# Other SBUF start addresses for the streamed operands of a two-layer encoder step

## The chip, the cores and the metric

One NeuronCore of one Trainium2 chip. The time is the device time of one execution in microseconds; the metric is the median over the runs.

## The reference

Two layers of a streaming encoder on 1056 tokens (1024 of a new stream, 32 of a running one) with 1024 features. Layer 0 mixes tokens by a gated short convolution, layer 1 by windowed means. Every layer then has a squared-ReLU MLP and a gated per-layer input. All of it is float32.

```python
def trunk(x, p, ...):
    for i in range(DEPTH):                       # DEPTH = 2
        y, nh = short_conv_mixer(...) if i % 2 == 0 else pool_mixer(...)
        h = layer_norm(ALPHA * x + y, ln1_g[i], ln1_b[i])
        r = jax.nn.relu(h @ mlp_w1[i])           # 1024 -> 4096
        f = (r * r) @ mlp_w2[i]                  # 4096 -> 1024
        e = (p[i] @ ple_w[i]) * jax.nn.sigmoid(h @ ple_gate_w[i])
        x = layer_norm(ALPHA * h + f + e, ln2_g[i], ln2_b[i])
    return x, ...

def short_conv_mixer(x, hist, w_in, conv_w, w_out):
    gb, gc, h = jnp.split(x @ w_in, 3, axis=-1)  # 1024 -> 3 x 1024
    ...
    y = (gb * conv) @ w_out
```

## The kernel before

**Layout.** Features lie on the 128 partitions, tokens along the row. The 1056 tokens are cut into NG = 3 groups of TG = 352, and the 1024 features into KD = 8 blocks. `blk(t, n, k)` is the block of group n and features k: 352 floats, 1408 bytes, one behind the other without a gap.

**Products in three parts.** Each operand is held as a high part (rounded to the format that TensorE takes in one pass) and a low part (the remainder): `x_hi`/`x_lo`, `h_hi`/`h_lo`, `r_hi`/`r_lo`, and `w_split[:, slot, 0 or 1, :]` for the weights. `triple` (L696 to L701) makes a product of three matmuls into one PSUM bank: high weights with the high part (L699), high weights with the low part (L700), low weights with the high part (L701). In each of them 128 columns of weights are loaded first, and then the 352 columns of the block are streamed through the array. `full_tile` (L703) runs `triple` over the eight blocks k of a group, 24 matmuls. A block's high part is thus streamed twice, with the low part between.

**Stages.**
- Input products of the convolution: `conv_in` (L708), from x, 8 feature blocks by 3 groups by 3 outputs; its first pass for group 0 is written out in pieces (L724, L728, L734) because x is still arriving.
- Then the plan, a list of steps that all engines walk in the same order: output products (`out`), gates (`gate`), MLP up (`up`) and pool products (`grp`) stream from h; MLP down (`down`, L854) and the token inputs (`ple`, L845) stream from r. An `up` step fills one block of r: ScalarE takes relu and square and rounds to `r_hi`, VectorE subtracts to `r_lo` (L1297). A `down` step makes four output blocks, each of CHUNK = 2 triples. r has three parts of two blocks, `rpart(t, n, f)` (L583), used in turn.
- Token inputs (`p`): a load of 704 floats per partition into a buffer of `w_raw`, split into the two blocks of a part of r by one copy of ScalarE (L887) and one subtraction of VectorE (`subtract_hi`, L614).
- Weights: 512 KB loads into `w_raw` by the SP queue (L635), split into one of six slots of `w_split` by ScalarE (L889) and VectorE (L616). Plan tables (`PLACES`, `REFILL_LATER`) say at which step each refill and each piece of the layer norms stands. The change touches none of them.

**Places in SBUF.** `place` (L410) hands out byte offsets in a partition's row, from a cursor that starts at 16640, or at an offset that is given. Several tensors share a place at different times: `acc` lies on `x_hi`; the windows of the pooling (`win_0` to `win_2`), r, `t` and `y_scaled_t` lie on `x_lo`; `x_raw` and `ln_squares` lie on `h_lo`; `u`, `gc` and `conv` lie in the slots 4 and 5 of `w_split` and behind. The program before places every block and every slice of 128 weights at a multiple of 128 bytes; since 1408 = 5.5 x 256, blocks with even number start at a multiple of 256 and those with odd number 128 past one.

Of the kernel before, what the change touches and what calls it, by code (L numbers as in the profile page):

```python
# [6 lines left out]
F32 = mybir.dt.float32  # L7

F32R = mybir.dt.float32r
ALU = mybir.AluOpType  # L10
ACT = mybir.ActivationFunctionType

P = 128
# [4 lines left out]
NG = 3  # L18
TG = TOKENS // NG
TAIL = PROMPT - (NG - 1) * TG  # L20
FF = 4 * D
CHUNK = 2
NCH = FF // P // CHUNK
PLE = 256
KP = PLE // P
# [5 lines left out]
EPS = 1e-5  # L31
U = 1024
GCOLS = KD * TG

# [363 lines left out]
def bass_streaming_trunk(nc, x_t, w_stream, p_t, vectors, conv_hist, pool_hist, y_t, conv_new, pool_new):  # L400
# [6 lines left out]
    with ExitStack() as ctx:  # L407
        cursor = [-(-nc.sbuf_base // 256) * 256]

        def place(name, shape, dt, at=None):  # L410
            size = 4
            for n in shape[1:]:
                size *= n
            size = -(-size // 32) * 32
            if at is None:
                at = cursor[0]
                cursor[0] += size
            return nc.alloc_sbuf_tensor_at(name, shape, dt, offset=at), at + size
# [7 lines left out]

        big = [P, NG * GCOLS]
        at1 = cursor[0]
        xh, _ = place("x_hi", big, F32R)
        acc, _ = place("acc", big, F32, at1)  # L430
        at2 = cursor[0]
        xl, end2 = place("x_lo", big, F32R)
        at3 = at2 + -(-GCOLS * 4 // 32) * 32
        WIN = HIST + TG + HIST
        w0, at = place("win_0", [P, 2, WIN], F32, at2)
        w1, at = place("win_1", [P, 2, WIN], F32, at)
        w2, at = place("win_2", [P, 2, WIN], F32, at)
        assert at <= at3
        row_hi, at = place("row_mean_hi", [P, 2 * CHUNK, P], F32R, at2)
        row_lo, at = place("row_mean_lo", [P, 2 * CHUNK, P], F32R, at)  # L440
        row_sum, at = place("row_sum", [P, 2 * CHUNK], F32, at)
        ident, at = place("identity", [P, P], F32, at)
        diag, at = place("rstd_diagonal", [P, 3, P], F32, at)
        assert at <= at3
        rh, at = place("r_hi", [P, NG * CHUNK * TG], F32R, at3)
        rl, at = place("r_lo", [P, NG * CHUNK * TG], F32R, at)
        tt, at = place("t", [P, 2, TG], F32, at)
        gs, at = place("y_scaled_t", [P, 2, TG], F32, at)
        assert at <= end2
        hh, at6 = place("h_hi", big, F32R)  # L450
        hl, at7 = place("h_lo", big, F32R)
        xraw, _ = place("x_raw", big, F32, at6)
        squares, _ = place("ln_squares", big, F32, at6)
        ws, _ = place("w_split", [P, 6, 2, U], F32R)
        UW = CH + PROMPT + CH + SAMPLE
        CW = TG + CH
        ub, at = place("u", [P, UW], F32, at7 + 4 * 2 * U * 4)
        gcs, at = place("gc", [P, NG, TG], F32, at)
        cv, at = place("conv", [P, NG, CW], F32, at)
        assert at <= at7 + 6 * 2 * U * 4  # L460
        raw, _ = place("w_raw", [P, 4, U], F32)
        w3, _ = place("win_3", [P, 2, WIN], F32)
        ones_r, _ = place("ones_r", [P, P], F32R)
        vec, _ = place("vec", [P, NV], F32)
        zeros, _ = place("zeros", [P, 2, HIST], F32)
        chist, _ = place("conv_history", [P, KD * CH], F32)
        phist, _ = place("pool_history", [P, KD, HIST], F32)
        cnew, _ = place("conv_state", [P, KD * 2 * CH], F32)
        tails, _ = place("tails", [P, 2, KD, HIST], F32)
        ones, _ = place("ones", [P, P], F32, cursor[0] - 2 * KD * HIST * 4)  # L470
        s_mean, _ = place("sum_mean", [P, TG], F32)
        s_var, at = place("sum_var", [P, TG], F32)
        std, _ = place("std", [P, TG], F32, at - -(-TG * 4 // 32) * 32)
        var, _ = place("var", [P, TG], F32)
        rstd, _ = place("rstd", [P, TG], F32)
# [16 lines left out]
        w_hi = sem("w_hi")  # L492
# [87 lines left out]
        def f32(ap):  # L580
            return ap.bitcast(F32)

        def rpart(t, n, f):  # L583
            at = (n * CHUNK + f) * TG
            return t[:, at:at + TG]

        def vcol(at):
            return vec[:, at:at + 1]
# [21 lines left out]
        def subtract_hi(eng, u, slot):  # L610

            if isinstance(slot, tuple):
                cols = slice(slot[1] * KP * TG, (slot[1] + 1) * KP * TG)
                ins = eng.tensor_tensor(rl[:, cols], raw[:, u.q, 0:KP * TG], f32(rh[:, cols]), ALU.subtract)  # L614
            else:
                ins = eng.tensor_tensor(ws[:, slot, 1, :], raw[:, u.q, :], f32(ws[:, slot, 0, :]), ALU.subtract)  # L616
            ins.then_inc(w_lo, 1)
# [262 lines left out]
        def _(act):  # L880
            def split_hi(u, slot, conds=()):
                act.wait_ge(raw_in[u.q], u.use * 16 + 16)
                for name, value in conds:
                    wait(act, sems[name], value)
                if isinstance(slot, tuple):
                    n = slot[1]
                    act.copy(rh[:, n * KP * TG:(n + 1) * KP * TG], raw[:, u.q, 0:KP * TG]).then_inc(w_hi, 1)  # L887
                else:
                    act.copy(ws[:, slot, 0, :], raw[:, u.q, :]).then_inc(w_hi, 1)  # L889

# [598 lines left out]
```

## Time and profile before

| | us |
|---|---|
| median of 2 runs | 2115.15 |
| lowest, highest | 2115.14, 2115.16 |
| span of the profiled execution, first to last instruction | 2114.6 |
| PE matmul busy | 2104.2 |
| PE weight load busy | 2101.3 |
| VectorE busy | 1266.8 |
| ScalarE busy | 821.8 |
| GpSimd busy | 74.8 |

The profiled execution has no time beside its span; the span is 0.5 us under the median of the runs, which also hold what lies around the instructions. The busy time of PE counts a matmul from its start to the modelled end of its results, so that consecutive matmuls overlap, and the mean duration of a group (some 320 ns) is not what one matmul costs. What one costs is seen from the starts in the timeline.

### The profile page before, as it was taken

The numbers are of one execution on the slowest core, as the hardware profiler recorded it, in microseconds if no ns is written. First come the engines' busy times: TensorE is split into PE (matmuls) and PEld (weight loads), VectorE is DVE, ScalarE is ACT, GpSimd is POOL, SyncE is SP. The second block draws the span as 40 slices with busy tenths as digits, with TensorE's granted clock in tenths as the row PEclk, the third lists the DMA queues.
The fourth block names the chain that finished last, engine by engine and source line by source line (L and its number), as shares of the span: only waits on it lengthen the run. The fifth ranks groups of instructions, "written<-read, shape, count | busy, mean of one in ns | idle before, by whom it ended". The sixth has DMA issues, their size and how long they took to land.

```text
span 2114.6 us, 31847 instructions
## 1 busy us (share of the span) xinstructions
PE 2104.2 (100%) x13214; PEld 2101.3 (99%) x13214; DVE 1266.8 (60%) x1892; ACT 821.8 (39%) x1287; POOL 74.8 (4%) x69
## 2 busy tenths in 40 slices
PE   9999999999999999999999999999999999999998
PEld 9999999999999999999999999999999999999998
DVE  5232357786454444444787877887875355645477
ACT  4222223663423322222544445555443324233345
POOL 0000000000000000000020002000300000000000
PEclk9999999999999999999999999999999999999999
DMA  4010241444122111111112343543222212122233
GB/s 175 30 60 30 69 129 48 130 129 142 63 85 96 51 50 41 40 60 41 60 54 87 100 147 120 168 139 121 62 77 92 69 51 70 51 80 80 64 107 133
DMA packets 54209, 179.68 MB, mean 85 GB/s; under 512 B 8128, under 2 KB 11328, under 8 KB 54080
## 3 DMA queue, kind: packets, MB, share of 16 engines
q1 hardware_dynamic: 51056, 177.15, 25.7%
q8 instruction: 95, 1.56, 0.3%
q10 hardware_dynamic: 3024, 0.70, 0.2%
q14 instruction: 34, 0.28, 0.0%
HBM read 173.36 MB, written 4.46 MB: 84 GB/s over the span
## 4 chain that ended last, share of the span: by engine, by line
PE 99%; DVE 0%; DMA 0%; SPq 0%; issue 0%; ACT 0%; DVEq 0%
PE ps L699 33%; PE ps L700 33%; PE ps L701 33%; DMA x_raw<-x_t 0%; DVE acc L1187 0%; PE ps L760 0%; PE ps L759 0%; PE ps L728 0%; PE ps L734 0%; SPq L641 0%; PE ps L797 0%; PE ps L724 0%; SPq L653 0%; DVE x_lo L1327 0%; SPq L649 0%
## 5 line engine op out<-in xcount | busy, mean ns | idle before, releaser
L699 PE MATMUL ps<-h_hi,w_split 128*128 128x352 f32 x2160 | 696.9, 323 | 0.4 <-DVE acc L1280 0.4
L700 PE MATMUL ps<-h_lo,w_split 128*128 128x352 f32 x2160 | 691.8, 320 | 0.0
L701 PE MATMUL ps<-h_hi,w_split 128*128 128x352 f32 x2160 | 691.6, 320 | 0.0
L699 PE MATMUL ps<-r_hi,w_split 128*128 128x352 f32 x1634 | 526.9, 322 | 0.0
L700 PE MATMUL ps<-r_lo,w_split 128*128 128x352 f32 x1634 | 523.1, 320 | 0.0
L701 PE MATMUL ps<-r_hi,w_split 128*128 128x352 f32 x1634 | 522.8, 320 | 0.0
L1311 DVE TENSOR_TENSOR acc<-acc,ps 128x352 f32<-128x352 f32 (+1 forms) x769 | 372.6, 516 | 125.5 <-PE ps L701 124.8
L616 DVE TENSOR_TENSOR w_split<-w_raw,w_split 128x1024 fp32r<-128x1024 f32 x291 | 356.5, 1247 | 99.2 <-ACT w_split L889 98.9
L699 PEld LDWEIGHTS ps<-h_hi,w_split 128*128 128x128 f32 x2160 | 405.0, 187 | 1.1 <-issue 1.0
L700 PEld LDWEIGHTS ps<-h_lo,w_split 128*128 128x128 f32 x2160 | 405.9, 188 | 0.0
L701 PEld LDWEIGHTS ps<-h_hi,w_split 128*128 128x128 f32 x2160 | 404.8, 187 | 0.0
L889 ACT CAST w_split<-w_raw 128x1024 fp32r<-128x1024 f32 x291 | 297.5, 1046 | 245.4 <-PE ps L701 243.8
L1297 DVE TENSOR_TENSOR r_lo<-t,r_hi 128x352 fp32r<-128x352 f32 x192 | 100.6, 524 | 380.0 <-ACT r_hi L1028 379.6
L700 PEld LDWEIGHTS ps<-r_lo,w_split 128*128 128x128 f32 x1634 | 306.9, 188 | 0.0
L699 PEld LDWEIGHTS ps<-r_hi,w_split 128*128 128x128 f32 x1634 | 306.4, 188 | 0.5 <-issue 0.3
L701 PEld LDWEIGHTS ps<-r_hi,w_split 128*128 128x128 f32 x1634 | 306.2, 187 | 0.0
L1022 ACT ACTIVATE t<-ps 128x352 f32<-128x352 f32 x192 | 89.3, 465 | 528.2 <-PE ps L701 526.6
L699 PE MATMUL ps<-x_hi,w_split 128*128 128x352 f32 x552 | 178.0, 322 | 0.0
L700 PE MATMUL ps<-x_lo,w_split 128*128 128x352 f32 x552 | 176.8, 320 | 0.0
L701 PE MATMUL ps<-x_hi,w_split 128*128 128x352 f32 x552 | 176.7, 320 | 0.0
L700 PEld LDWEIGHTS ps<-x_lo,w_split 128*128 128x128 f32 x552 | 103.7, 188 | 0.0
L699 PEld LDWEIGHTS ps<-x_hi,w_split 128*128 128x128 f32 x552 | 103.5, 188 | 0.0
(133 smaller groups left out, 1198.5 us busy)
## 6 DMA issues: line engine op xcount, KB each, us to landing
w_raw<-w_stream SPq DMA_DIRECT2D x315, 512.0 KB, 3.5
x_raw<-x_t SPq DMA_DIRECT2D x4, 704.0 KB, 8.7
y_t<-acc SPq DMA_DIRECT2D x4, 704.0 KB, 4.1
w_raw<-p_t SPq DMA_DIRECT2D x6, 352.0 KB, 2.8
y_t<-acc SPq DMA_DIRECT2D x7, 176.0 KB, 2.0
w_raw<-w_stream SPq DMA_DIRECT2D x3, 256.0 KB, 6.1
x_raw<-x_t SPq DMA_DIRECT2D x4, 176.0 KB, 4.5
x_raw<-x_t SPq DMA_DIRECT2D x2, 352.0 KB, 6.8
```

The source lines that it names most:

```text
L616: ins = eng.tensor_tensor(ws[:, slot, 1, :], raw[:, u.q, :], f32(ws[:, slot, 0, :]), ALU.subtract)
L699: pe.matmul(out, wh, mov_h, start=first, stop=False)
L700: pe.matmul(out, wh, mov_l, start=False, stop=False)
L701: return pe.matmul(out, wl, mov_h, start=False, stop=last)
L889: act.copy(ws[:, slot, 0, :], raw[:, u.q, :]).then_inc(w_hi, 1)
L1022: act.activation(t, ps[:, step.bank, 0:TG], ACT.Relu).then_inc(a_free, 1)
L1297: dve.tensor_tensor(rpart(rl, *r), tt[:, step.bank, :], f32(rpart(rh, *r)), ALU.subtract).then_inc(r_ready, 1)
L1311: dve.tensor_tensor(cols, cols, ps[:, bank, at:end], ALU.add).then_inc(b_free, 1)
```

## The change

It moves tensors in SBUF; what is computed, the order of instructions on each engine and the waits stay. Gaps of 64, 64, 128 and 128 bytes go in front of `x_lo`, `h_hi`, `h_lo` and `w_split`. A block of r takes RS = 368 floats (1472 bytes) of place, of which 352 are used, r begins 1024 bytes earlier within the place of `x_lo`, and `r_lo` begins 128 bytes behind the end of `r_hi`. The two instructions that fill both blocks of a part at once write through `rpair`, two runs of 352 instead of one of 704. `x_raw` and `ln_squares` move with `h_lo`.

Start of each streamed tensor in a partition, in bytes, and its remainder by 256 (even block, odd block):

| tensor | before | even, odd | after | even, odd |
|---|---|---|---|---|
| `x_hi` | 16640 | 0, 128 | 16640 | 0, 128 |
| `x_lo` | 50432 | 0, 128 | 50496 | 64, 192 |
| `h_hi` | 84224 | 0, 128 | 84352 | 128, 0 |
| `h_lo` | 118016 | 0, 128 | 118272 | 0, 128 |
| `r_hi` parts 0 and 2 | 61696 | 0, 128 | 60736 | 64, 0 |
| `r_hi` part 1 | 64512 | 0, 128 | 63680 | 192, 128 |
| `r_lo` parts 0 and 2 | 70144 | 0, 128 | 69696 | 64, 0 |
| `r_lo` part 1 | 72960 | 0, 128 | 72640 | 192, 128 |
| `w_split`, every slice of 128 weights | 151808 | 0 | 152192 | 128 |
| `w_raw`, every buffer | 200960 | 0 | 201344 | 128 |

```diff
--- before.py
+++ after.py
@@ -31,6 +31,7 @@
 EPS = 1e-5
 U = 1024
 GCOLS = KD * TG
+RS = TG + 16
 
 
 
@@ -428,9 +429,10 @@
         at1 = cursor[0]
         xh, _ = place("x_hi", big, F32R)
         acc, _ = place("acc", big, F32, at1)
+        cursor[0] += 64
         at2 = cursor[0]
         xl, end2 = place("x_lo", big, F32R)
-        at3 = at2 + -(-GCOLS * 4 // 32) * 32
+        at3 = at2 + -(-GCOLS * 4 // 32) * 32 - 1024
         WIN = HIST + TG + HIST
         w0, at = place("win_0", [P, 2, WIN], F32, at2)
         w1, at = place("win_1", [P, 2, WIN], F32, at)
@@ -442,16 +444,20 @@
         ident, at = place("identity", [P, P], F32, at)
         diag, at = place("rstd_diagonal", [P, 3, P], F32, at)
         assert at <= at3
-        rh, at = place("r_hi", [P, NG * CHUNK * TG], F32R, at3)
-        rl, at = place("r_lo", [P, NG * CHUNK * TG], F32R, at)
+        rh, at = place("r_hi", [P, NG * CHUNK * RS], F32R, at3)
+        rl, at = place("r_lo", [P, NG * CHUNK * RS], F32R, at + 128)
         tt, at = place("t", [P, 2, TG], F32, at)
         gs, at = place("y_scaled_t", [P, 2, TG], F32, at)
         assert at <= end2
+        cursor[0] += 64
         hh, at6 = place("h_hi", big, F32R)
-        hl, at7 = place("h_lo", big, F32R)
-        xraw, _ = place("x_raw", big, F32, at6)
-        squares, _ = place("ln_squares", big, F32, at6)
-        ws, _ = place("w_split", [P, 6, 2, U], F32R)
+        cursor[0] += 128
+        hl, _ = place("h_lo", big, F32R)
+        xraw, _ = place("x_raw", big, F32, at6 + 128)
+        squares, _ = place("ln_squares", big, F32, at6 + 128)
+        cursor[0] += 128
+        ws, at7 = place("w_split", [P, 6, 2, U], F32R)
+        at7 -= 6 * 2 * U * 4
         UW = CH + PROMPT + CH + SAMPLE
         CW = TG + CH
         ub, at = place("u", [P, UW], F32, at7 + 4 * 2 * U * 4)
@@ -581,8 +587,11 @@
             return ap.bitcast(F32)
 
         def rpart(t, n, f):
-            at = (n * CHUNK + f) * TG
+            at = (n * CHUNK + f) * RS
             return t[:, at:at + TG]
+
+        def rpair(t, n):
+            return t[:, n * KP * RS:(n + 1) * KP * RS].rearrange("p (k t) -> p k t", k=KP)[:, :, 0:TG]
 
         def vcol(at):
             return vec[:, at:at + 1]
@@ -610,8 +619,8 @@
         def subtract_hi(eng, u, slot):
 
             if isinstance(slot, tuple):
-                cols = slice(slot[1] * KP * TG, (slot[1] + 1) * KP * TG)
-                ins = eng.tensor_tensor(rl[:, cols], raw[:, u.q, 0:KP * TG], f32(rh[:, cols]), ALU.subtract)
+                tokens = raw[:, u.q, 0:KP * TG].rearrange("p (k t) -> p k t", k=KP)
+                ins = eng.tensor_tensor(rpair(rl, slot[1]), tokens, f32(rpair(rh, slot[1])), ALU.subtract)
             else:
                 ins = eng.tensor_tensor(ws[:, slot, 1, :], raw[:, u.q, :], f32(ws[:, slot, 0, :]), ALU.subtract)
             ins.then_inc(w_lo, 1)
@@ -884,7 +893,7 @@
                     wait(act, sems[name], value)
                 if isinstance(slot, tuple):
                     n = slot[1]
-                    act.copy(rh[:, n * KP * TG:(n + 1) * KP * TG], raw[:, u.q, 0:KP * TG]).then_inc(w_hi, 1)
+                    act.copy(rpair(rh, n), raw[:, u.q, 0:KP * TG].rearrange("p (k t) -> p k t", k=KP)).then_inc(w_hi, 1)
                 else:
                     act.copy(ws[:, slot, 0, :], raw[:, u.q, :]).then_inc(w_hi, 1)
```

## Rows read from the trace of the kernel before

**Rows 1.** The page, parts 1 and 2: busy time, and the granted clock in 40 slices.

```profile
PE 2104.2 (100%) x13214; PEld 2101.3 (99%) x13214; DVE 1266.8 (60%) x1892; ACT 821.8 (39%) x1287; POOL 74.8 (4%) x69
PEclk9999999999999999999999999999999999999999
```

**Rows 2.** The page, part 4: the chain that ended last, by engine.

```profile
PE 99%; DVE 0%; DMA 0%; SPq 0%; issue 0%; ACT 0%; DVEq 0%
```

**Rows 3.** Waits of PE, whole span: total us, times, longest.

```profile
PE ps L871 <- POOL zeros L1351: 1.1, 1, 1.1
PE ps L724 <- ACT x_hi L1052: 0.9, 1, 0.9
PE ps L790 <- DVE ln_squares L1173: 0.6, 1, 0.6
PE ps L699 <- DVE acc L1280: 0.4, 1, 0.4
PE ps L797 <- DVE rstd_diagonal L1184: 0.3, 1, 0.3
PE ps L728 <- DVE x_lo L1327: 0.2, 1, 0.2
```

**Rows 4.** The page, part 5: groups of L699, count | busy us, mean ns.

```profile
L699 PE MATMUL ps<-h_hi,w_split 128*128 128x352 f32 x2160 | 696.9, 323 | 0.4 <-DVE acc L1280 0.4
L699 PE MATMUL ps<-r_hi,w_split 128*128 128x352 f32 x1634 | 526.9, 322 | 0.0
L699 PE MATMUL ps<-x_hi,w_split 128*128 128x352 f32 x552 | 178.0, 322 | 0.0
```

**Rows 5.** Timeline of PE from 699.69 us: start us, duration us, line, operation.

```profile
699.69 0.32 PE L699 MATMUL ps<-h_hi,w_split 128*128 128x352 f32 x1
699.85 0.32 PE L700 MATMUL ps<-h_lo,w_split 128*128 128x352 f32 x1
700.01 0.32 PE L701 MATMUL ps<-h_hi,w_split 128*128 128x352 f32 x1
700.16 0.32 PE L699 MATMUL ps<-h_hi,w_split 128*128 128x352 f32 x1
700.33 0.32 PE L700 MATMUL ps<-h_lo,w_split 128*128 128x352 f32 x1
700.48 0.32 PE L701 MATMUL ps<-h_hi,w_split 128*128 128x352 f32 x1
700.64 0.32 PE L699 MATMUL ps<-h_hi,w_split 128*128 128x352 f32 x1
...
727.33 0.32 PE L699 MATMUL ps<-r_hi,w_split 128*128 128x352 f32 x1
```

**Rows 6.** Windows: 1000 to 1700 us, PE busy (x), PEld, DVE, ACT, POOL, clock.

```profile
1000.00:1700.00 700.00, 700.00 (x4404) 699.50 (x4404) 518.51 (x728) 332.50 (x522) 50.99 (x32) 1.00 0.31 99
```

**Rows 7.** Timeline of PE at the last tile: start us, duration us, line, operation.

```profile
2100.80 0.28 PE L699 MATMUL ps<-r_hi,w_split 128*128 128x256 f32 x1
...
2101.52 0.21 PE L699 MATMUL ps<-r_hi,w_split 128*128 128x96 f32 x1
2101.56 0.27 PE L700 MATMUL ps<-r_lo,w_split 128*128 128x96 f32 x1
...
2102.01 0.28 PE L701 MATMUL ps<-r_hi,w_split 128*128 128x96 f32 x1
```

**Rows 8.** Timeline of PE from 323.17 to 327.01 us, first and last row.

```profile
323.17 0.32 PE L699 MATMUL ps<-h_hi,w_split 128*128 128x352 f32 x1
...
327.01 0.32 PE L699 MATMUL ps<-h_hi,w_split 128*128 128x352 f32 x1
```

**Rows 9.** Split of the token inputs, and the weight loads (us to landing).

```profile
L887 ACT CAST r_hi<-w_raw x6: 780/780/784, 376.9 to 1594.6; 128x704 fp32r<-128x704 f32 x6
L614 DVE TENSOR_TENSOR r_lo<-w_raw,r_hi x6: 881/887/895, 381.0 to 1595.4; 128x704 fp32r<-128x704 f32 x6
w_raw<-w_stream SPq DMA_DIRECT2D x315, 512.0 KB, 3.5
```

## Prediction

> **What bounds the kernel now.** I read the page's first two parts, then the chain and the waits, to see whether any engine but TensorE sets the time. TensorE's matmul side is busy for 2104.2 of 2114.6 us, and its granted clock is 9 or more in every slice, so it runs at the 2.4 GHz level [rows 1]. The chain of waits puts 99% of the span on PE [rows 2]. PE's waits for other engines are six and sum to 3.5 us [rows 3]. VectorE (60%) and ScalarE (39%) have slack, and the kernel's only long resource is the row of 13,214 matmuls. Of these, 3 x (2160 + 1634 + 552) = 13,038 come from `triple` (L699, L700, L701), nearly all 352 columns wide: 6,480 stream h, 4,902 stream r, 1,656 stream x [rows 4].
>
> The next question is what one matmul costs. The 320 ns of the groups is no cost, since two matmuls overlap in the record; the cost is the distance from one start to the next, which I call the gap. In the timeline of one stretch [rows 5] the starts come in sets of six: three matmuls on one block (high, low, high), then three on the next. From 699.69 to 727.33 us there are 29 sets, 174 gaps: 27.64 us / 174 = 158.9 ns. Over 700 us with pooling work beside it 4404 records touch the window, two of them already running at its start, which gives 700 / 4402 = 159.0 ns [rows 6]. So the gap hardly depends on what the other engines do.
>
> 352 columns at 2.4 GHz stream in 146.7 ns, so 12.2 ns of each gap is not streaming. The last tile says what kind of time that is [rows 7]: six matmuls of 256 columns take 0.72 us, 120 ns each, against 106.7 ns of columns, so 13.3 ns over. 96 columns fewer save 38.9 ns, against 40 of pure streaming. The 12 ns is thus a cost per matmul, not per column. With 96 columns the gap is (2102.01 - 2101.56) / 4 = 112 ns, although the columns need only 40; there the weight loads set the pace. At 352 columns that pace has 47 ns to spare. 12.2 ns x 13,038 = 159 us is everything that this change could touch.
>
> **Does an address matter at all?** I averaged each of the six gaps over the 30 sets that begin from 699.69 to 727.33 us; rows 5 show the first set and the start of the last. In their order: 160.0, 161.3, 155.3, 161.7, 155.0, 159.8 ns. The second and the fifth are the same step: the low stream ends, the high one of the same block begins, with the weights' low half. They differ by 6.3 ns. What differs between the blocks is where they lie: 1408 bytes are 5.5 x 256, so even blocks start at 0 and odd ones at 128 past a multiple of 256. Address phases are worth some nanoseconds per matmul, in both directions. A second stretch warns that they are not all: between 323.17 and 327.01 us the same instructions on the same addresses go 24 gaps in 3.84 us, 160.0 ns each [rows 8]. So the same layout can run in more than one rhythm.
>
> The Trainium skill, "TensorE: Matmul & The Clock Gate", Back-to-back issue gap, gives an isolated gap of columns over 2.4 GHz plus about 2.5 ns; "SBUF — State Buffer", Who interferes with whom, gives TensorE two read ports, one for the moving operand and one for weights, and says that it never waits on anyone. By those two pages a place in SBUF is worth nothing and the time stays at 2115. The trace disagrees with the first figure (12.2 ns instead of 2.5), and the 6.3 ns between equal steps is not in the page's picture.
>
> **The change part by part.** The instruction order of all engines is the same, and so are all waits. Only two groups change shape: the six copies (L887) and six subtractions (L614) that split a token input now write two runs of 352 with 64 bytes between them instead of one of 704. They take 780 and 887 ns now [rows 9]; even twice that would be 10 us on engines with hundreds of microseconds to spare, and PE has no listed wait on them. I take nothing. If the cover were gone, the first of the six could hold PE for under a microsecond.
>
> DMA destinations: w_raw moves from a multiple of 256 to 128 past one. A load lands after 3.5 us at the median [rows 9] and loads are issued well ahead, since no wait of PE on a weight is listed [rows 3]. Nothing again; a load 1 us slower would not show.
>
> What is left is the gap, by stage.
>
> - h, 6,480 matmuls. All three of a block's streams used to start at one phase. Now the low part lies 128 off the high, and since a stream moves the phase by 128 from start to end, every matmul starts at the phase (mod 256) at which the one before it ended, and the weights keep their distance from the high part. In the old order two of six steps continue in this way, the third and the sixth: (155.3 + 159.8) / 2 = 157.6 ns. The other four mean 159.5. I take 157.6 for all: 1.25 ns x 6,480 = 8.1 us saved. Bounds: 155.0 gives 25 us saved, 161.7 gives 18 us lost.
> - r, 4,902 matmuls. Blocks start at 64 and 0, or 192 and 128, high and low parts alike, with weights at 128. The trace has no stream that starts 64 off, so I bound by its extremes: 155.0 saves 19 us, 161.7 costs 14 us. I take the middle between the best gap and the present mean, 157.0: 1.9 ns x 4,902 = 9.3 us saved. It is the weakest number here. The reason to lean to a gain is that four of the present six gaps are near the top of the seen range, so a mix of phases has more room below than above.
> - x, 1,656 matmuls. The low part is 64 off the high. Same treatment, 1.9 ns x 1,656 = 3.1 us saved; bounds 6.4 us saved, 4.7 us lost.
> - The first 19 us and the last 12 us have few matmuls and waits of another kind: nothing.
>
> Sum: 8.1 + 9.3 + 3.1 = 20.5 us saved. The span is 2114.6 us and the median of the runs 2115.15, 0.5 more, so the forecast is 2115.15 - 20.5 = 2094.6, said as 2095 us, 1.0% faster. All parts at their best: 25 + 19 + 6.4 = 50 us, 2065. All at their worst: 37 us, 2152.
>
> **Rivals.** A: *no change*. The per-matmul cost is a fixed handoff, and the rhythm settles to the same average on any layout. For it: the stage on x, the one on h and the one on r all have equal groups now (means of 322 or 323 ns at L699) [rows 4]. Against it: 6.3 ns between equal steps. It gives 2115.
>
> B: *the half line*. If a stream is fetched in pieces of 128 bytes, 1408 bytes from a multiple of 128 are 11 whole pieces, and from 64 past one they touch 12. Place: half of r's matmuls (2,451) and the third of x's that reads the low part (552). Price: at most one piece of 16 more columns, 6.7 ns, so 20 us. It decides once the 64-byte phases cost more than h gains; with h's 8.1 us kept it is 2127, with h at the slower rhythm of rows 8 (160.0, 7 us lost) 2142. I put it at 2127. For it: nothing in the trace starts on an odd 64, so nothing excludes it. Against it: at 256 columns the excess is the same as at 352, so there is no sign of a fetch that runs at its limit.
>
> C: *the best gap everywhere*. Each step falls on the phase that costs 155.0 or less: 50 us saved or more, 2065, perhaps 2060. For it: 155 is seen once in every three steps or so. Against it: the steps are coupled. A short gap (155) is always followed by a longer one in rows 5, as if the start had to wait for a turn that comes round; then an average near the minimum needs every step to fit.
>
> The Trainium skill, "SBUF — State Buffer", Specifications, says lines are 16 bytes and each crossing costs. All starts here, old and new, are multiples of 64 bytes and all streams contiguous, so by it B is excluded too; no row tests it.
>
> **How the numbers follow.** Forecast (a gain of 0.2 to 2%) 0.44; A 0.20; B (any loss over 0.2%) 0.20, of which 0.04 over 2%; C 0.16. About 2% is what a measurement of this kernel can tell from no change. Faster by over 2% (below 2073) is C, 0.16; slower by over 2% (above 2157) needs more than the worst gap seen, at most 0.04; within 2% is the rest, 0.80. For eight in ten I go from 2066, where C's bulk lies, to 2128, just past B.
>
> **What would show it.** Right for h: in the timeline of a stretch on h the six gaps become equal or alternate in two values, with a mean below 158.9. Right for r and x: the same sets of six below 158.9. B: gaps of L700 on x_lo, and of r's first blocks, up by some nanoseconds while their odd partners stay. A: sets of six at 953 to 960 ns in all three stages. Wrong altogether: a new wait on PE, for r_lo, x_lo or a weight, or a clock below 9 in a slice. Stages may go opposite ways; the sum of three signs is what this rests on.

## The result, and the profile after

The changed kernel takes 2140.03 us (median of 2 runs, 2139.28 to 2140.77) against 2115.15: ratio 1.0119, 95% interval 1.0094 to 1.0143. It is 1.2% slower, where 1.0% faster was forecast, and it lies above the range's end of 2128. A second series beside the kernel before gave 2141.05 against 2116.00 us, ratio 1.0118 (1.0101 to 1.0135).

The page of the changed kernel, parts 1, 2 and 4, in the order of [rows 1, 2]:

```profile
span 2139.0 us, 31847 instructions
PE 2128.6 (100%) x13214; PEld 2126.3 (99%) x13214; DVE 1269.7 (59%) x1892; ACT 822.4 (38%) x1287; POOL 74.9 (3%) x69
PEclk9999999999999999999999999999999999999999
PE 99%; DVE 0%; DMA 0%; SPq 0%; issue 0%; ACT 0%; DVEq 0%
```

Nothing else became a bound: PE holds 99% of the chain as before, the clock is the same, and the waits of PE sum to 3.4 us (3.5 before). VectorE and ScalarE are busy for 3 and 1 us more. Three of PE's waits, from the list (total us, times, longest):

```profile
PE ps L733 <- ACT x_hi L1061: 0.5, 1, 0.5
PE ps L708 <- DVE acc L1289: 0.4, 1, 0.4
PE ps L733 <- DVE w_split L1334: 0.3, 1, 0.3
```

The last of them, on the weights' first pieces, was not in the list before, and the prediction had named a new wait on a weight as a sign of being wrong. It is 0.3 us, on the line (L733, L724 before) that waited 0.9 us for x_hi before and waits 0.5 us for it now, so it adds nothing.

The copies into the two runs of r were to cost nothing, and did: L623 is L614 of before, where its mean was 888 ns.

```profile
L623 DVE TENSOR_TENSOR r_lo<-w_raw,r_hi 128x704 fp32r<-128x704 f32 x6 | 5.3, 887 | 1.0 <-ACT r_hi L896 1.0
```

The time is in the gaps. Windows of the changed kernel, PE busy (x records), then PE's weight loads and the other engines in the same form, the granted clock, the DMA share and GB/s; the three stretches are input products (x), output products (h), and a mix of h and r:

```profile
100.00:280.00 180.00, 180.00 (x1120) 180.00 (x1119) 59.42 (x102) 39.08 (x63) 11.79 (x15) 1.00 0.13 47
300.00:370.00 70.00, 70.00 (x435) 70.00 (x434) 52.13 (x66) 23.02 (x26) 0.00 (x0) 1.00 0.25 81
1000.00:1700.00 700.00, 700.00 (x4353) 699.71 (x4352) 516.83 (x723) 330.72 (x519) 51.09 (x32) 1.00 0.30 99
```

The first two windows in the kernel before:

```profile
100.00:280.00 180.00, 180.00 (x1135) 180.00 (x1134) 60.21 (x105) 39.31 (x64) 11.91 (x16) 1.00 0.14 47
300.00:370.00 70.00, 70.00 (x439) 70.00 (x439) 53.45 (x69) 22.49 (x26) 0.00 (x0) 1.00 0.23 74
```

With the two matmuls that already run at a window's start left out, the stage on x went from 180 us / 1133 = 158.9 ns per matmul to 180 / 1118 = 161.0, and the mix from 159.0 [rows 6] to 700 / 4351 = 160.9. From 300 to 370 us, h alone, it is 70 / 433 = 161.7. In the kernel before this stretch is one of the slower ones on h, 70 / 437 = 160.2, where the mean over all of h is 159.0. The starts show this without counting. In the timeline of the stage on x, 25 sets of six lie between the first row and the last, 24.16 us / 150 = 161.1 ns; a set takes 0.966 us where it took 0.953 [rows 5]:

```profile
100.18 0.33 PE L709 MATMUL ps<-x_lo,w_split 128*128 128x352 f32 x1
100.34 0.33 PE L710 MATMUL ps<-x_hi,w_split 128*128 128x352 f32 x1
100.50 0.32 PE L708 MATMUL ps<-x_hi,w_split 128*128 128x352 f32 x1
100.66 0.32 PE L709 MATMUL ps<-x_lo,w_split 128*128 128x352 f32 x1
100.82 0.32 PE L710 MATMUL ps<-x_hi,w_split 128*128 128x352 f32 x1
100.99 0.32 PE L708 MATMUL ps<-x_hi,w_split 128*128 128x352 f32 x1
101.14 0.33 PE L709 MATMUL ps<-x_lo,w_split 128*128 128x352 f32 x1
...
124.34 0.33 PE L709 MATMUL ps<-x_lo,w_split 128*128 128x352 f32 x1
```

On h, 144 gaps in 23.28 us are 161.7 ns:

```profile
318.16 0.32 PE L708 MATMUL ps<-h_hi,w_split 128*128 128x352 f32 x1
...
341.44 0.32 PE L710 MATMUL ps<-h_hi,w_split 128*128 128x352 f32 x1
```

Here is the loss by stage, each mean taken over all starts of the stage in the trace (gaps above 205 ns left out), before and after: x 158.9 and 161.1, h 159.0 and 161.6, r 158.9 and 160.0. Times 1,656, 6,480 and 4,902 matmuls this is 3.6 + 17.0 + 5.4 = 26.0 us; the long gaps (above 205 ns, at waits) sum to 1.6 us less. The spans differ by 24.4.

The groups of part 5 hide it almost wholly, since each duration covers two matmuls [rows 4]:

```profile
L708 PE MATMUL ps<-h_hi,w_split 128*128 128x352 f32 x2160 | 699.0, 324 | 0.4 <-DVE acc L1289 0.4
L708 PE MATMUL ps<-r_hi,w_split 128*128 128x352 f32 x1634 | 527.5, 323 | 0.0
L708 PE MATMUL ps<-x_hi,w_split 128*128 128x352 f32 x552 | 177.9, 322 | 0.0
```

### The profile page after: what moved, and what is told of

It is laid out like the page before. It is cut to its first block, busy times and chain, and to the rows that moved or that the text cites. A ratio compares the mean times of both kernels' runs of the same rounds, so it can differ in the third digit from the quotient of the medians.

```text
span 2139.0 us, 31847 instructions
## 1 busy us (share of the span) xinstructions
PE 2128.6 (100%) x13214; PEld 2126.3 (99%) x13214; DVE 1269.7 (59%) x1892; ACT 822.4 (38%) x1287; POOL 74.9 (3%) x69
## 4 chain that ended last, share of the span: by engine, by line
PE 99%; DVE 0%; DMA 0%; SPq 0%; issue 0%; ACT 0%; DVEq 0%
PE ps L708 33%; PE ps L710 33%; PE ps L709 33%; DMA x_raw<-x_t 0%; DVE acc L1196 0%; PE ps L769 0%; PE ps L768 0%; PE ps L737 0%; PE ps L743 0%; SPq L650 0%; PE ps L806 0%; PE ps L733 0%; SPq L662 0%; DVE x_lo L1336 0%; SPq L658 0%
## 5 line engine op out<-in xcount | busy, mean ns | idle before, releaser
L708 PE MATMUL ps<-h_hi,w_split 128*128 128x352 f32 x2160 | 699.0, 324 | 0.4 <-DVE acc L1289 0.4
L709 PE MATMUL ps<-h_lo,w_split 128*128 128x352 f32 x2160 | 699.1, 324 | 0.0
L710 PE MATMUL ps<-h_hi,w_split 128*128 128x352 f32 x2160 | 698.7, 323 | 0.0
L708 PE MATMUL ps<-r_hi,w_split 128*128 128x352 f32 x1634 | 527.5, 323 | 0.0
L710 PE MATMUL ps<-r_hi,w_split 128*128 128x352 f32 x1634 | 527.0, 323 | 0.0
L708 PEld LDWEIGHTS ps<-h_hi,w_split 128*128 128x128 f32 x2160 | 407.5, 189 | 1.0 <-issue 0.8
L710 PEld LDWEIGHTS ps<-h_hi,w_split 128*128 128x128 f32 x2160 | 407.5, 189 | 0.0
L708 PEld LDWEIGHTS ps<-r_hi,w_split 128*128 128x128 f32 x1634 | 307.1, 188 | 0.1
L710 PEld LDWEIGHTS ps<-r_hi,w_split 128*128 128x128 f32 x1634 | 306.7, 188 | 0.0
L710 PE MATMUL ps<-x_hi,w_split 128*128 128x352 f32 x552 | 178.8, 324 | 0.0
L708 PE MATMUL ps<-x_hi,w_split 128*128 128x352 f32 x552 | 177.9, 322 | 0.0
L710 PEld LDWEIGHTS ps<-x_hi,w_split 128*128 128x128 f32 x552 | 104.8, 190 | 0.0
L708 PEld LDWEIGHTS ps<-x_hi,w_split 128*128 128x128 f32 x552 | 104.0, 188 | 0.0
```

What stands on the lines that cost most here:

```text
L708: pe.matmul(out, wh, mov_h, start=first, stop=False)
L709: pe.matmul(out, wh, mov_l, start=False, stop=False)
L710: return pe.matmul(out, wl, mov_h, start=False, stop=last)
```

## The experiments

Four readings of the two traces stood ahead of the first four runs. **S**: a block's three streams should begin at the same remainder by 256, and alternating costs. **W**: the weights' remainder costs. **P**: streams that start at an odd 64 fetch half a piece more, rival B of the prediction. **R**: the rhythm depends on everything before it, so that any move may end in another one. After these runs R was sharpened to **K**, which the later expectations use: the gap does not belong to a step; the matmuls settle in one of a few rhythms that a layout allows, and the moment of entry picks one.

**One part alone.** The edits on the kernel before:

```diff
 # h_only
         hh, at6 = place("h_hi", big, F32R)
-        hl, at7 = place("h_lo", big, F32R)
-        xraw, _ = place("x_raw", big, F32, at6)
-        squares, _ = place("ln_squares", big, F32, at6)
-        ws, _ = place("w_split", [P, 6, 2, U], F32R)
+        cursor[0] += 128
+        hl, _ = place("h_lo", big, F32R)
+        xraw, _ = place("x_raw", big, F32, at6 + 128)
+        squares, _ = place("ln_squares", big, F32, at6 + 128)
+        cursor[0] += 128
+        ws, at7 = place("w_split", [P, 6, 2, U], F32R)
+        at7 -= 6 * 2 * U * 4
 # w_only
-        hl, at7 = place("h_lo", big, F32R)
+        hl, _ = place("h_lo", big, F32R)
...
         squares, _ = place("ln_squares", big, F32, at6)
-        ws, _ = place("w_split", [P, 6, 2, U], F32R)
+        cursor[0] += 128
         ws, at7 = place("w_split", [P, 6, 2, U], F32R)
         at7 -= 6 * 2 * U * 4
+        cursor[0] += 128
 # r_only: RS, rpair, rpart and both splits as in the change, and
-        at3 = at2 + -(-GCOLS * 4 // 32) * 32
+        at3 = at2 + -(-GCOLS * 4 // 32) * 32 - 960
-        rh, at = place("r_hi", [P, NG * CHUNK * TG], F32R, at3)
-        rl, at = place("r_lo", [P, NG * CHUNK * TG], F32R, at)
+        rh, at = place("r_hi", [P, NG * CHUNK * RS], F32R, at3)
+        rl, at = place("r_lo", [P, NG * CHUNK * RS], F32R, at + 128)
```

> The kernel before with h_lo alone moved 128 bytes against h_hi; weights, x and r keep their old remainders. Theory S (a block's three streams should begin at the same remainder by 256; alternating costs): the stretches on h go from 158.9 to about 161.6 ns per matmul as in the changed kernel, x and r stay at 158.9, total about 2115 + 6480 x 2.7 ns = 2132 us. Rival W (what costs is the weights' remainder of 128): nothing moves, 2115 us. Rival R (the rhythm depends on everything before it, so that any move of any tensor may end in 160 or 161): all three stages move, 2115 to 2130 us.

> The kernel before with w_split alone moved by 128 bytes. Theory S: the weights' remainder does not count, 158.9 ns in all stages, 2115 us. Rival W: weights and streams collide by their distance, every stage moves to about 161, 2115 + 13038 x 2 ns = 2141 us. Rival R: anything between 2115 and 2130 us.

> The kernel before with r alone as in the change (stride of 1472 bytes, remainders 64 and 0, 192 and 128), weights at remainder 0. Theory S: r's three streams of a block still share a remainder, so r costs little, 0 to 1 ns per matmul: 2115 to 2120 us. Theory P (half pieces: a stream that starts at an odd 64 costs up to 6.7 ns more): half of 4902 matmuls, up to 2131 us. If r alone is a gain, the loss of the changed kernel lies in h and x alone: below 2113 us.

h_only: 2140.89 us, ratio 1.0121 (1.0107 to 1.0135). Its windows, 100 to 280, 300 to 370 and 1000 to 1700 us:

```profile
100.00:280.00 180.00, 180.00 (x1135) 180.00 (x1134) 60.65 (x105) 39.90 (x65) 12.75 (x17) 1.00 0.14 47
300.00:370.00 70.00, 70.00 (x435) 70.00 (x435) 52.82 (x68) 22.51 (x26) 0.00 (x0) 1.00 0.23 74
1000.00:1700.00 700.00, 700.00 (x4346) 699.74 (x4345) 514.75 (x721) 329.23 (x518) 50.77 (x32) 1.00 0.31 98
```

The stage on x keeps its 1135 records, h alone is at 161.7 ns as in the changed kernel. So far S. But r, which had not moved, went from 158.9 to 160.5 ns (all its gaps), and the total is 26 us, not 17: 2140.89 lies above what S (2132), W (2115) and R (2115 to 2130) had said. A stage that is left alone changes when the one beside it in time is moved: h and r alternate every few tiles.

w_only: 2141.92 us at the median, ratio 1.0102 (1.0059 to 1.0146; it is formed with all four executions, of which one was much faster). In the profiled execution, 2141.82 us, all stages are at 161:

```profile
100.00:280.00 180.00, 180.00 (x1119) 180.00 (x1118) 59.50 (x102) 39.08 (x63) 11.77 (x15) 1.00 0.14 47
300.00:370.00 70.00, 70.00 (x436) 70.00 (x435) 52.25 (x66) 23.04 (x26) 0.00 (x0) 1.00 0.25 81
1000.00:1700.00 700.00, 700.00 (x4354) 699.71 (x4353) 516.85 (x723) 330.71 (x519) 50.76 (x32) 1.00 0.31 99
```

That is what W had said (2141), and S had excluded; three of the four lie above R's 2130. But of its four executions one took 2120.14 us and the others 2141.8 to 2143.4, at one granted clock (0.998), while seven executions of the kernel before in the same series took 2114.5 to 2116.5. The same program, with the same addresses, comes in two times that are 22 us apart. A fixed price for a remainder can't do that; a rhythm that is picked at the start can.

r_only: 2121.97 us, ratio 1.0032 (1.0018 to 1.0046), x and h as before:

```profile
100.00:280.00 180.00, 180.00 (x1135) 180.00 (x1134) 61.04 (x106) 40.08 (x64) 13.23 (x17) 1.00 0.15 47
1000.00:1700.00 700.00, 700.00 (x4388) 699.74 (x4387) 519.10 (x728) 331.03 (x519) 50.75 (x32) 1.00 0.31 98
```

r's own gaps mean 160.3 ns, 1.4 more than before, 7 us. S had said 2120 at most. Theory P asked for up to 16 us and for slow gaps where a stream starts at an odd 64. Among r's twelve kinds of steps those from 64 to 64 (161.8) are slow, but those between 0 and 0 (160.8 and 160.0) are slow too, and those from 192 to 192, also an odd 64, are not (159.3 and 158.4), so P has little left.

**A map of layouts.** The kernel keeps the launch and outputs zeros. TensorE streams 48 matmuls per layout in the order of `triple`, twice over eight blocks, each layout four times, after one short matmul:

```python
for stride, w, h, l in CONFIGS:
    for rep in range(REPS):
        cols = (96, 224, 288, 160)[rep]
        pe.matmul(ps[:, 4, 0:cols], mk[:, 0:P], mk[:, 0:cols], start=True, stop=True)
        last = run(stride, w // 4, h // 4, l // 4, 2 * (rep % 2))
```

> No part of the model is computed: the output is zeros. TensorE alone streams 54 layouts one after the other, each four times as 48 matmuls of 352 columns in the order high, low, high over eight blocks, after one short matmul of 96, 224, 288 or 160 columns that changes the moment of the start. Theory S: layouts with the low part at the high part's remainder take 158.9 ns per matmul whatever the weights' remainder, those 128 off take 161.6. Rival W: the mean follows the distance of weights and streams. Theory P: layouts whose low part is 64 off are slower by 2 ns in the mean, those 32 off by as much or more. Shifting all three tensors by 64 or 128 together changes nothing if only distances count; if the place itself counts, it does. The best layout should be below 157 ns if the offsets were worth choosing at all.

The timeline of the map at the layout that the change gives to h (weights 0, high 0, low 128, stride 1408); L147 is the short matmul. Each line of "..." leaves out matmuls of one start:

```profile
148.36 0.32 PE L139 MATMUL ps<-lo,wt 128*128 128x352 f32 x1
...
155.96 0.27 PE L147 MATMUL ps<-mark 128*128 128x224 f32 x1
156.06 0.33 PE L139 MATMUL ps<-hi,wt 128*128 128x352 f32 x1
...
163.82 0.29 PE L147 MATMUL ps<-mark 128*128 128x288 f32 x1
163.95 0.32 PE L139 MATMUL ps<-hi,wt 128*128 128x352 f32 x1
...
171.71 0.23 PE L147 MATMUL ps<-mark 128*128 128x160 f32 x1
...
171.98 0.32 PE L139 MATMUL ps<-lo,wt 128*128 128x352 f32 x1
...
179.42 0.21 PE L147 MATMUL ps<-mark 128*128 128x96 f32 x1
```

From 148.36 to 155.96 us are 47 gaps: 161.7 ns. The next two starts have 48 gaps in 7.76 us each, 161.7 again. The fourth start, on the same layout, does 47 gaps from 171.98 to 179.42 us: 158.3 ns. Only what stood before it differs (the second and the fourth start write the same two PSUM banks as well). Some of the 54 layouts, the mean of 42 gaps of each start in ns, from the fifth to the forty-sixth:

```
stride  weights  high  low    four starts
1408    0        0     0      158.9  158.9  159.1  158.9    (kernel before)
1408    0        0     128    161.7  161.7  161.7  158.3    (change, h)
1408    128      128   256    161.7  161.7  161.7  161.7    (the same, 128 further)
1408    128      0     0      160.0  161.1  158.9  158.9    (w_only)
1408    128      0     64     161.0  161.1  161.1  161.0    (change, x)
1408    0        0     64     161.1  161.0  161.0  161.0
1408    0        0     32     161.1  162.2  161.9  161.1
1408    64       64    64     158.9  158.9  161.1  158.9    (all at an odd 64)
1408    64       0     64     162.0  162.2  161.9  162.0
1536    0        0     0      160.0  160.0  161.1  160.0
1536    128      0     0      166.7  158.3  158.3  158.4
```

Five things follow. First, the layout of w_only has rhythms of 158.9, 160.0 and 161.1. Its profiled execution ran mostly at 161.1; the one of 2120.14 us has no trace, and its 5 us over the kernel before are 159.3 ns per matmul by estimate, which a mix of the two faster rhythms would give. Second, all three tensors at an odd 64 run at 158.9 in three starts of four; P is out. Third, no start of this map is below 158.3: the best that any of these choices could give is 0.4%. Fourth, the layout says which rhythms are open, and for many layouts it is one: in 30 of the 54 the four starts lie within 0.5 ns, the layout that the change gives to x among them (161.0 to 161.1). There the cost is a fixed one, as far as four starts can tell. Fifth, many means are not arbitrary. In 115 of the 216 starts the sum of six or of twelve consecutive gaps stays the same from the fifth gap on, within 2 ns, and every one of these sums, over twelve gaps at the latest, is a whole multiple of 6.667 ns: over six gaps 953.3, 960, 966.7, 973.3 and 1000 ns (143, 144, 145, 146 and 150 times), over twelve, among others, 1900 and 1940 for the two rhythms of the alternating layout (285 and 291 times). The other starts, with offsets that are multiples of 64 too, give means in between that I did not resolve. 6.667 ns is the time of 16 columns at 2.4 GHz. I read a rhythm as a sequence of gaps that comes back to the same place on a grid of that step; the sums fit this, and no run shows the grid itself.

The map also excludes the traffic of the other engines as the cause: from 30 us on it has no instruction of VectorE, ScalarE or GpSimd and a DMA share of 0.00, and the means of the kernels come out again.

**The other way round.** The changed kernel with h's part undone, x's part alone, and everything 128 further:

```diff
 # no_h, on the kernel after
         hh, at6 = place("h_hi", big, F32R)
-        cursor[0] += 128
         hl, _ = place("h_lo", big, F32R)
-        xraw, _ = place("x_raw", big, F32, at6 + 128)
-        squares, _ = place("ln_squares", big, F32, at6 + 128)
-        cursor[0] += 128
+        xraw, _ = place("x_raw", big, F32, at6)
+        squares, _ = place("ln_squares", big, F32, at6)
         ws, at7 = place("w_split", [P, 6, 2, U], F32R)
 # x_only, on the kernel before (at3 64 less, so that r stays)
+        cursor[0] += 64
         at2 = cursor[0]
...
+        cursor[0] += 192
         hh, at6 = place("h_hi", big, F32R)
 # shift_all, on the kernel before
+        cursor[0] += 128
         at1 = cursor[0]
```

> The changed kernel with its part on h undone: h_hi, h_lo and the weights all at remainder 128 by 256, x and r as in the change. Theory K (the gap settles in one of a few rhythms that a layout allows, and the moment of entry picks one): h runs at 158.9, 160.0 or 161.1 as one layout did in the map, never at 161.67; x at 161.1 and r near 160 as in the changed kernel; total 2115 + 3.6 + 5 + (0 to 14) = 2124 to 2138 us. Theory S (only the alternation between high and low part costs, always the same): 2124 us in every run.

> The kernel before with x_lo alone 64 bytes off, all else at its old remainders. Theory K: the input stage at 161.0 as that layout in the map (all four starts), 1656 x 2.1 ns = 3.5 us, 2118.5 us, and a later stage may enter another rhythm of its own, which adds steps of whole microseconds. Theory P (half pieces): the low part's gaps alone grow, by up to 6.7 ns, the others stay.

> The kernel before with every tensor 128 bytes further, so that all distances stay. Theory K: the same rhythms as before are open (158.9, 160.0, 161.1), and the run takes 2115 us if it falls into the same ones; some runs may take 10 to 25 us more. Rival A2 (the place itself counts, remainder 128 is bad): slower in every run, by the same amount.

no_h: 2122.14 us, ratio 1.0033 (1.0021 to 1.0044). Windows of x, h, and the mix:

```profile
100.00:280.00 180.00, 180.00 (x1119) 180.00 (x1119) 59.59 (x102) 39.08 (x63) 11.79 (x15) 1.00 0.14 47
300.00:370.00 70.00, 70.00 (x443) 70.00 (x442) 52.95 (x67) 23.05 (x26) 0.00 (x0) 1.00 0.26 81
1000.00:1700.00 700.00, 700.00 (x4395) 699.61 (x4395) 520.28 (x732) 331.62 (x520) 50.86 (x32) 1.00 0.30 98
```

Over all its gaps h is back at 159.0 as before; in the window it is at 70 / 441 = 158.7, faster than the kernel before in the same stretch (160.2). x stays at 161.1, r at 159.6. 3.6 + 3.4 = 7.0 us, as measured. So h's part of the change carries 18 of its 25 us. K had allowed h three rhythms here and said 2124 to 2138; h took the fast one, the total came out 2 us below K's range and the same distance from the 2124 of S, so this run alone doesn't part K from S.

x_only: 2119.08 us, ratio 1.0018 (1.0008 to 1.0027): 3.8 us more, 3.6 expected from 161.1 ns on x. No other stage moved. P fails here too. In the order of `triple` over two blocks, the six gaps on x were 160.8, 161.6, 156.0, 160.8, 155.1 and 159.2 ns in the kernel before and are 159.2, 164.1, 160.9, 159.2, 160.9 and 162.4 now: the low part's own gaps (the second and the fifth) grow, but the third and the sixth grow as well and the first and the fourth shrink.

shift_all: 2114.92 us, ratio 0.9998 (0.9989 to 1.0008); none of its ten executions took the 10 to 25 us more that K had thought possible. Moving everything by 128 is worth nothing, only distances count:

```profile
100.00:280.00 180.00, 180.00 (x1135) 180.00 (x1134) 60.62 (x105) 39.90 (x65) 12.73 (x17) 1.00 0.14 47
1000.00:1700.00 700.00, 700.00 (x4403) 699.58 (x4402) 517.65 (x727) 332.52 (x522) 50.72 (x32) 1.00 0.31 99
```

**A second map** varied the order of the three matmuls, the remainder of the low weights, and the moment of start more finely, eight starts each.

> No part of the model is computed: the output is zeros. A second map, 28 layouts with eight starts each, the short matmul ahead having 280 to 350 columns. It varies the order of the three matmuls of a block, the remainder of the low weights against the high ones, and the stride. Theory K: each layout shows two or three distinct mean gaps over its eight starts, each of them a multiple of 6.667 ns over the six or twelve matmuls of its period; the layout of the changed kernel on h shows 158.3 in some starts and 161.67 in others, that of before 158.9 in most. If some order or low-weight remainder gives 158.3 or less in all eight starts, it is the better kernel. Rival F (fixed cost per step): one value per layout.

The layout of the change on h showed 158.3 in one start of eight and 161.7 in seven (with the weights 128 off, 158.3 in two and 161.6 to 161.8 in six). The layout of before showed 158.9 twice, 160.0 or 160.1 three times and 161.1 three times, so my "158.9 in most" was a miss: with freely varied moments the old layout is no safer than a draw. With both halves of the weights 128 off, the layout of w_only, the starts gave the same three rhythms in much the same shares (158.9 or 159.0 three times, 160.0 twice, 161.1 three times). So the 27 us of w_only are not shown to be a price of the weights' place: the same rhythms are open with and without the move, and what differs is which one the kernel enters. That the weights' place can change the rhythms themselves is shown at the stride of 1536 bytes: with the weights at 0 the starts gave 160.0 and 161.1 only, with the weights at 128 only 158.3 and 166.7, in twelve starts each over both maps. With the low weights 128 off the high ones it stayed between 158.9 and 159.9 in all starts, a mean of 159.3. With the low stream as the last of the three matmuls, the alternating layout gave 158.9 to 161.2. Rival F, one fixed value per layout, fell: in 21 of the 28 layouts the starts lie more than 0.5 ns apart. K's own sentence on the multiples of 6.667 ns held in part: 125 of the 224 starts repeat over six or twelve gaps and are such multiples, the others did not settle that way. None gave 158.3 in every start. The layout with the low weights 128 off the high ones was steadier than the old one, but the kernel before already runs at 158.9 to 159.0, so it promised no gain, and it was not built.

**A try at the fast rhythm.** Stride 1536 had run at 158.3 in six of eight starts of the second map (and 166.7 in two), and r has room for it. On the kernel before, with `rpair`, `rpart` and both splits as in the change, and no gap in front of `r_lo`:

```diff
+RS = TG + 32
-        at3 = at2 + -(-GCOLS * 4 // 32) * 32
+        at3 = at2 + -(-GCOLS * 4 // 32) * 32 - 1920
```

> The kernel before with r alone at a stride of 1536 bytes, so that all its blocks begin at remainder 128 while the weights stay at 0; h and x as before. In the second map that layout ran at 158.3 ns in six starts and at 166.7 in two. Theory K: if r's short tiles (six matmuls, between longer ones on h) settle in the faster rhythm, 4902 x 0.6 ns = 3 us less, 2112; if in the slower, up to 38 us more; a tile of six may be too short to settle at all, then about 2115 with r's mean between the two.

2149.90 us, ratio 1.0159 (1.0142 to 1.0176). r's gaps mean 164.1 ns (single gaps from 155 to 167), nearer to the slow rhythm of 166.7, and h, unmoved, went to 160.4: 25 + 9 us. The window of the mix:

```profile
100.00:280.00 180.00, 180.00 (x1135) 180.00 (x1134) 60.65 (x105) 39.91 (x65) 12.74 (x17) 1.00 0.15 47
1000.00:1700.00 700.00, 700.00 (x4346) 699.56 (x4345) 516.31 (x723) 331.20 (x519) 50.76 (x32) 1.00 0.31 99
```

A share of good starts in a map is not the share that a program meets. The likely reason, not tested, is that in the program the entry to r's tiles always comes from the same few places.

> The changed kernel once more, beside the kernel before on one chip. Theory K: 2140 us with a spread of 1 to 3 us between executions, where the kernel before has its own, because r and h change rhythm at moments that differ from run to run; h at 161.6, x at 161.1, r at 160. No execution below 2130.

It gave 2140.28 to 2141.21 us over four executions, a spread of 0.9 us, with the stage means of the first profile.

**The moment alone, inside the kernel.** On the changed kernel, no address is touched:

```diff
-            def full_tile(bank, slot, src_h, src_l, n):
+            def full_tile(bank, slot, src_h, src_l, n, nudge=0):
+                if nudge:
+                    pe.matmul(ps[:, bank, 0:nudge], ws[:, slot, 0, 0:P], blk(src_h, n, 0)[:, 0:nudge], start=True, stop=True)
...
-                    full_tile(step.a % 2, step.slot, hh, hl, step.n).then_inc(out_full, 1)
+                    full_tile(step.a % 2, step.slot, hh, hl, step.n, 280 + 10 * (step.a % 8)).then_inc(out_full, 1)
```

and the same for the gate tiles.

> The changed kernel, with one extra matmul of 280, 290, ... or 350 columns ahead of each of the 24 output tiles and 48 gate tiles on h; its result is overwritten. It costs 72 x about 0.15 us = 11 us and shifts the moment at which the tile's 24 matmuls start. Theory K: among these 72 tiles some run at 158.3 ns per matmul and others at 161.7, as the two maps show for this layout, where without the extra matmuls the stretch from 300 to 370 us is at 161.67 throughout; total 2140 + 11 us less up to 5. Rival F (fixed cost of the layout): all tiles stay at 161.6.

Timeline of two neighbouring tiles (L714 is the extra matmul, L710 the third and the last of a tile's 24):

```profile
317.39 0.29 PE L714 MATMUL ps<-h_hi,w_split 128*128 128x280 f32 x1
...
317.84 0.32 PE L710 MATMUL ps<-h_hi,w_split 128*128 128x352 f32 x1
...
321.23 0.32 PE L710 MATMUL ps<-h_hi,w_split 128*128 128x352 f32 x1
321.39 0.29 PE L714 MATMUL ps<-h_hi,w_split 128*128 128x290 f32 x1
...
321.84 0.32 PE L710 MATMUL ps<-h_hi,w_split 128*128 128x352 f32 x1
...
325.17 0.32 PE L710 MATMUL ps<-h_hi,w_split 128*128 128x352 f32 x1
```

After 280 columns the tile's 21 gaps from 317.84 to 321.23 us are 161.4 ns each; after 290 columns, from 321.84 to 325.17, 158.6. (The starts are printed to 10 ns, so these two are good to half a nanosecond.) Of the 72 tiles 12 ran at 158.3 (mean of 22 gaps) and 60 at 161.4 to 161.9. The share hangs on the moment: after 290 columns six of nine tiles were fast, after 300 three of nine, after 280, 310 and 340 one of nine each, after 320, 330 and 350 none. The total was 2150.41 us in the one execution, the extra matmuls' cost included. In the undisturbed kernel that stretch is at 161.7 throughout, and over the whole kernel 4 of 265 runs of 24 matmuls on h go at 158.3.

## Why the prediction was wrong

**What bounds the kernel: right.** A row of matmuls, 12.2 ns each beyond the columns, nothing behind it. No wait, no copy and no load took part, as costed at nothing (the waits sum to 3.4 us, the copies take 887 ns).

**That addresses matter: right, in the wrong place.** The prediction showed that the second and the fifth gap of a set differ by 6.3 ns and read a price per step out of it. The step that failed is in the sum for h: "In the old order two of six steps continue in this way ... I take 157.6 for all". A gap is not a property of a step. Gaps in order in ns, each line beginning at a high stream (L699, L708 after), from the starts as the traces hold them:

```
before, from 699.69 us   161.0  161.7  155.7  161.0  155.0  159.0
before, from 323.17 us   159.0  158.0  161.0  160.0  160.0  162.0
after, from 318.16 us    159 164 165 159 159 164 165 158 160 164 165 158
```

The third and the sixth step, which the prediction took for the good ones, take 155.7 and 159.0 ns in one stretch of the kernel before and 161.0 and 162.0 in the other, on the same addresses. In the changed kernel, where every step continues its predecessor's phase, they take 158 to 165 ns, not 157.6. Only the mean over a period means anything, and by the maps a layout leaves few values open for it. The new layout leaves 158.3 and 161.7, and h entered the slower one nearly everywhere. (The six means of the prediction were formed from starts rounded to 10 ns and are up to 1 ns off; the second and the fifth differ by 6.7 ns, not 6.3. Nothing hangs on this.) 8.1 us saved became 17.0 lost. The prediction did note that "the steps are coupled", as an argument against rival C, and did not apply it to its own term.

**r and x: sizes without ground.** 157.0 for both was "the middle between the best gap and the present mean", which assumed that means can lie anywhere between single gaps. They measured 160.0 and 161.1: 5.4 and 3.6 us lost instead of 9.3 and 3.1 saved. x's value is the one that its layout gave in every start of the map; r's is a mean over short tiles that no map isolates. In the two maps' 82 layouts no mean below 158.3 was seen but for one start at 157.8, so the reason to lean to a gain ("more room below than above") was the wrong way round: the kernel before already sat within 0.4% of the best rhythm that came more than once.

**The rival on the losing side had the sign, not the mechanism.** B gave 2127 and 2142 "with h at the slower rhythm of rows 8"; 2140 lies beside the second figure by luck: half pieces are excluded by the map and by the gaps of x_only, and h went to 161.6, not 160.0. The warning was in rows 8: the same instructions at the same addresses in two rhythms, 158.9 and 160.0. Read to the end it says that a mean is one of several on the same layout and may come out higher on a new one.

**The range.** The sum of worst gaps, 2152, was worked out and then cut to 2128. The worst case by stage (161.7 for all) was nearly what h and x took.

**The chances** of faster or slower by 2% rested on gaps of a few nanoseconds, and the kernel stayed within 2%. The 0.44 on a gain and the 0.16 on C were on the wrong side of 2115.

Open stays what the grid is. The runs show that the rhythms go with the distances between streams and weights and with the moment: moving a stream alone (h_only, x_only), the weights alone (stride 1536 in the maps) or nothing but the moment (nudge) changes the mean, moving all together does not. Whether it is a turn of the memory or of the engine no run here tells. It was not tried without weight loads between matmuls. Nor is it shown why the kernel before, whose layout has three rhythms open, took 2113.9 to 2116.6 us in all of its 39 executions.

## What to carry to other kernels

When TensorE runs back to back and each matmul costs a few nanoseconds more than its columns, the excess can be a rhythm: average over a whole period of the loop, in several executions and from several moments of entry, before giving single gaps a price. Offsets between the streams and the weights cost up to 2.5% of a matmul here (at a stride of 1536 bytes up to 4.9%, 166.7 ns) and gave 0.4% at best but for one start at 0.7%, never in every start. Tensors on one remainder were as good as anything in the kernels; in the second map the low weights 128 off the high ones were steadier (159.3 on the average of eight starts, against 160.2). A layout that is left alone changes too when its neighbour in time does, so parts can't be added up: h alone cost 26 us, r alone 7 and x alone 4, the whole change 25.

## What the hardware showed that I had not expected

- Two rhythms for one program: w_only took 2120.14 us in one execution and 2141.8 to 2143.4 in three, at a granted clock of 0.998 each time. Every other kernel's executions in one series lie within 3 us.
- The steps: where the gaps repeat (240 of the 440 starts of both maps), sets of six matmuls of 352 columns take 946.7, 953.3, 960.0, 966.7, 973.3 or 1000 ns, sets of twelve also 1900 to 1953.3, 1940 most often, all whole multiples of 6.667 ns.
- Where the weights lie against the streams changes the pace: at a stride of 1536 bytes, weights 128 bytes off turned 160.0 and 161.1 ns into 158.3 and 166.7 (twelve starts each). The Trainium skill, "SBUF — State Buffer", Who interferes with whom, gives the moving operand and the weight load independent read ports and says that TensorE never waits on anyone; by that no distance should count, and these starts disagree. The Trainium skill, "TensorE: Matmul & The Clock Gate", Back-to-back issue gap, gives 2.5 ns beyond the columns for a matmul by itself. Here, in rows of weight load and matmul, the excess is 11.6 to 15 ns in the rhythms of x and h, and it depends on the distances.
- Shifting everything by 128 bytes changed nothing, 0.9998 (0.9989 to 1.0008).
